# Boundaries between sub-layers: the low part of the first tile's upper half is made by GpSimd between its last two roots and multiplied by TensorE ahead of the last tile's transposes

## The reference

```python
def rmsnorm(x, g):
    xf = x.astype(jnp.float32)
    y = xf * lax.rsqrt(jnp.mean(xf * xf, axis=-1, keepdims=True) + EPS)
    return y.astype(x.dtype) * g

def ffn_sublayer(x, shift, scale, gate, g_pre, g_post, w_in, w_out):
    h = modulate(rmsnorm(x, g_pre), shift, scale)
    a, b = jnp.split(h @ w_in, 2, axis=-1)
    h = (jax.nn.silu(a) * b) @ w_out
    return x + FFN_RES * gate * rmsnorm(h, g_post)
```

## Time and profile before

| what | us |
|---|---|
| median of 3 runs | 3028.7 |
| lowest and highest | 3026.51, 3028.95 |
| the profiled execution | 3027.37 |
| its span in the profile | 3025.3 |
| PE matmuls busy in it | 2971.6 |
| DVE busy | 2194.8 |
| ACT busy | 1152.7 |
| POOL busy | 594.1 |

### The profile page before, as it was taken

One profiled execution on the slowest core, in us unless ns is written; L12 is line 12 of the kernel. 1 busy time (PEld: TensorE's weight loads), 2 busy tenths in 40 slices (PEclk: granted clock), 3 DMA queues, 4 the chain that ended last, 5 costly groups with the idle time before them and its releaser, 6 DMA issues.

```text
span 3025.3 us, 46963 instructions
## 1 busy us (share of the span) xinstructions
PE 2971.6 (98%) x18482; PEld 2753.4 (91%) x18482; DVE 2194.8 (73%) x2831; ACT 1152.7 (38%) x1966; POOL 594.1 (20%) x586
## 2 busy tenths in 40 slices
PE   7999999999999999999999999999999999999999
PEld 6999888999999998999899999979999999888998
DVE  6888678887877656888787576768887888775444
ACT  4222564223322434222422365553224222664222
POOL 1111212112211212112211144541122112211001
PEclk9999999999999999999999999999999999999999
DMA  8666435665665445666566443327675766333443
GB/s 299 209 211 215 142 84 192 209 209 167 210 209 172 117 135 167 219 211 197 181 209 202 132 117 93 105 89 236 208 215 166 221 211 197 111 80 119 126 127 96
DMA packets 565935, 515.61 MB, mean 170 GB/s; under 512 B 43013, under 2 KB 499286, under 8 KB 563926
## 3 DMA queue, kind: packets, MB, share of 16 engines
q1 hardware_dynamic: 565158, 512.37, 55.8%
q10 hardware_dynamic: 560, 0.25, 0.0%
HBM read 509.31 MB, written 3.24 MB: 169 GB/s over the span
## 4 chain that ended last, share of the span: by engine, by line
PE 89%; issue 4%; DVE 2%; POOL 2%; ACT 1%; DMA 1%; SPq 0%; DVEq 0%; POOLq 0%; ACTq 0%
PE bank L1671 19%; PE bank L1673 18%; PE bank L1672 18%; PE bank L1720 9%; PE bank L1722 9%; PE bank L1721 9%; PE bank L1688 2%; PE bank L1695 1%; PE bank L614 1%; PE bank L639 1%; DMA ada_first<-w_ada 1%; PE bank L1753 1%; POOL hg_kr L1491 1%; POOL small L2358 0%; POOL small L2363 0%
## 5 line engine op out<-in xcount | busy, mean ns | idle before, releaser
L1671 PE MATMUL bank<-h_hi,w_hi 128*128 128x384 f32 x3328 | 1120.6, 337 | 0.0
L1673 PE MATMUL bank<-h_hi,w_lo 128*128 128x384 f32 x3328 | 1114.9, 335 | 0.0
L1672 PE MATMUL bank<-h_lo,w_hi 128*128 128x384 f32 x3328 | 1113.6, 335 | 0.0
L1925 ACT ACTIVATE w_hi<-raw 128x1024 fp32r<-128x1024 f32 x646 | 680.8, 1062 | 1032.8 <-PE bank L1673 483.6
L2081 DVE TENSOR_TENSOR w_lo<-raw,w_hi 128x1024 fp32r<-128x1024 f32 x648 | 812.2, 1276 | 330.6 <-ACT w_hi L1925 325.8
L2108 DVE SCALAR_TENSOR_TENSOR fold<-ada_raw,cond,fold 128x1024 f32<-128x1024 f32 x462 | 638.5, 1438 | 0.1
L1671 PEld LDWEIGHTS bank<-h_hi,w_hi 128*128 128x128 f32 x3328 | 625.2, 188 | 10.9 <-ACT tmp L1944 1.6
L1672 PEld LDWEIGHTS bank<-h_lo,w_hi 128*128 128x128 f32 x3328 | 625.3, 188 | 6.1
L1673 PEld LDWEIGHTS bank<-h_hi,w_lo 128*128 128x128 f32 x3328 | 625.0, 188 | 0.0
L2399 POOL TENSOR_TENSOR h_lo<-tmp,h_hi 128x384 fp32r<-128x384 f32 x176 | 280.4, 1593 | 1741.3 <-DVE h_hi L2142 1741.3
L1720 PE MATMUL bank<-w_hi,h_hi 128*128 128x512 f32 x1056 | 415.4, 393 | 0.0
(11 more groups left out here) (204 smaller groups left out, 2425.7 us busy)
## 6 DMA issues: line engine op xcount, KB each, us to landing
raw<-w_ffn_in SPq DMA_DIRECT2D x352, 512.0 KB, 5.0
ada_raw<-w_ada SPq DMA_DIRECT2D x264, 512.0 KB, 4.2
raw<-w_ffn_out SPq DMA_DIRECT2D x176, 512.0 KB, 4.6
raw<-w_hgrn_in SPq DMA_DIRECT2D x40, 512.0 KB, 3.9
g_rows<-g_dram SPq DMA_DIRECT2D x12, 1024.0 KB, 6.7
raw<-w_attn_qkv SPq DMA_DIRECT2D x24, 512.0 KB, 5.9
raw<-w_conv_in SPq DMA_DIRECT2D x24, 512.0 KB, 4.9
ada_first<-w_ada SPq DMA_DIRECT2D x16, 512.0 KB, 10.9
```

Of the source, the lines that this page charges most:

```text
L1671: mm(out, wh, h_hi[:, k, :], start=(k == 0), stop=False)
L1672: mm(out, wh, h_lo[:, k, :], start=False, stop=False)
L1673: last = mm(out, wl, h_hi[:, k, :], start=False, stop=(k == DC - 1))
L1925: A(w_hi[:, b % RING, :], raw[:, b % RAW, :], ACT.Copy).then_inc(w_hi_made, 1)
```

## The change

Three edits, all for the boundaries e = 1 to 11:

- POOL runs `lo_half(e, 0, 1)`, the low part of the upper half of tile 0, between `out_root(e, 2)` and `y_root(e, 2)`. Three `lo_half` remain after the last root, in the order tile 1 upper, tile 0 lower, tile 1 lower.
- PE runs a new `first_low(e)` after `first_tile(e)` and ahead of the transposes of tile 2: it waits for that one low part and does 8 matmuls (2 banks by 4 chunks) of 128 columns, `w_hi` by `h_lo` of tile 0.
- In `first_blocks` the 8 matmuls of the upper half's low part take only tiles 1 and 2 (256 columns) in place of 384. The 8 of the lower half stay at 384.

```diff
             for half in (1, 0):
                 pe.wait_ge(h_lo_made, (NT - 1) * (2 * (s + 1) - half))
                 pe.wait_ge(h_lo_last, 2 * (s + 1) - half)
+                low = rest if half == 1 and s > 0 else slice(0, T)
                 for j, bank in enumerate(banks):
                     for k in range(4 * half, 4 * half + 4):
-                        last = mm(psum[bank][:, 0:T], w_hi[:, (b0 + j) % RING, k * P:(k + 1) * P], h_lo[:, k, :],
+                        last = mm(psum[bank][:, low], w_hi[:, (b0 + j) % RING, k * P:(k + 1) * P], h_lo[:, k, low],
                                   start=False, stop=(k == 3), skip_group_check=True)
...
+        def first_low(s):
+
+            pe.wait_ge(h_lo_made, (NT - 1) * 2 * s + 1)
+            for j, bank in enumerate(first_banks(s)):
+                for k in range(4, 8):
+                    mm(psum[bank][:, 0:P], w_hi[:, (first_block[s] + j) % RING, k * P:(k + 1) * P], h_lo[:, k, 0:P],
+                       start=False, stop=False, skip_group_check=True)
...
                 first_tile(e)
+                first_low(e)
                 turn_normed(e, 2)
...
                 for t in range(NT):
                     out_root(e, t)
+                    if t == NT - 1:
+                        lo_half(e, 0, 1)
                     y_root(e, t)
 
                 gp.wait_ge(h_high_made, 2 * (NT * e + NT - 2) + 2)
-                for half in (1, 0):
-                    for t in range(NT - 1):
-                        lo_half(e, t, half)
+                lo_half(e, 1, 1)
+                lo_half(e, 0, 0)
+                lo_half(e, 1, 0)
```

## The result

| | before | after |
|---|---|---|
| median of 8 runs, us | 3027.85 | 3035.32 |
| lowest and highest | 3024.36, 3029.26 | 3031.17, 3040.16 |
| the profiled execution's span | 3025.3 | 3037.5 |
| PE busy in it | 2971.6 | 2981.4 |
| POOL busy | 594.1 | 587.0 |

What follows compares the result with a forecast made beforehand. PE, busy 98% of the span, bounds the kernel, with a slackless chain from `out_root` to tile 2's transposes at boundaries. Terms -5.0 + 11.2 + 0.6 = +6.8 us on 3028.7 gave 3035.5, range 3028 to 3040.

Steps and rivals of the forecast that it cites:

- Term 2: At each boundary, DVE's additions to y of tile 2 wait for POOL's moved low part: +11.2 us in all.
- the pair at 300.8 us: POOL and DVE subtractions started 0.07 us apart; DVE's took 2.03 us for 1.22, as if begun 0.13 before POOL's end.
- the third pair: At the boundary's end, POOL's subtraction takes 1.75 us for 1.27 and DVE's 1.78 for 0.68, 1.1 more.
- The second: Pair at 58.47 us: POOL takes 1.98 us for some 1.0, DVE's next, at 59.50, 2.03 for 1.28.
- The estimate of 1.24 us: Delay of DVE's addition by the skill page's rule, blocked engine going on about 115 ns after the holder's end.
- rival 1: POOL's low part and DVE's additions don't collide: no delay, 3020.6 to 3023.7 us, faster; chance 0.14.
- rival 2: POOL and DVE share rather than take turns, about 0.5 us delay a boundary: 3029 us, no change; chance 0.12.
- Term 1: Eight low-part matmuls behind L1688 narrowed from 384 to 256 columns: 0.45 us a boundary, -5.0 us, counted in full.
- The 13.85 of the prediction: Time from `first_tile` to L1671 after the change where the clock stays: 13.25 + 1.05 - 0.45 = 13.85 us.
- The end of the boundary: POOL's fourth low part and DVE's `lo_last` disturbed each other, hidden with 0.2 us to spare; nothing gained or lost.
- Term 3: Boundaries with a stretch at PE's lower clock: 3 to 4 expected for 3, +0.6 us, bounds -3.1 and +8.
- rival 3: PE's clock falls in most boundaries, its quiet stretch being later and longer: +13.8 us, 3042.5; chance 0.07.

Runs made afterwards that it cites:

- experiment 1: Kernel before with only GpSimd's order changed, one low part ahead of the last `y_root`, TensorE as before: 3047.33 us, ratio 1.0063 against the kernel before.
- experiment 3: Kernel before with only two of the low part's four chunks made ahead of the last `y_root`, TensorE as before: 3037.56 us, ratio 1.0037.
- experiment 4: Changed kernel, but GpSimd begins the early low part only after both additions to y of tile 2: 3026.69 us, ratio 0.9994 against the kernel before.
- experiment 5: ScalarE's rounding of the sixth weight block moved behind the first Silu in FFN boundaries: 3033.45 us on the changed kernel, 3028.08 on the one before.
- experiment 2: Changed kernel with GpSimd's old order, the 8 added matmuls multiplying the high part instead: 3024.78 us, ratio 0.9991 against the kernel before.

## Why the prediction was right, and where it was not

Forecast 3035.5 with slower the likeliest case, measured 3035.32, slower.

- **Term 2, the delay of the chain,** was +11.2 us, 1.05 a boundary. Measured 5.63 - 4.69 = 0.94 in ten boundaries and 0.59 in the ninth: 10.0 us. The turn was taken as forecast, POOL first. The value worked out from the pair at 300.8 us, 1.0, was nearer than the 1.05 taken between it and the 1.1 of the third pair. Not "all" pairs lie there. The second would have given what was measured: there DVE's instruction ends as if begun at 59.50 + 2.03 - 1.28 = 60.25, 0.20 us before POOL's end at 58.47 + 1.98 = 60.45, and with 0.20 in place of 0.13 the sum gives 0.94. DVE went on 0.21 us before GpSimd's recorded end here. Experiments 1, 3 and 4 show the cause: the delay comes with the low part alone, shrinks by just what POOL's instruction shrinks, and is gone from the addition when POOL starts later. The Trainium skill's rule ("SBUF — State Buffer", section "SBUF: two separate sides"), that the one that starts first holds the shared ports for its whole instruction, agrees with these runs in kind. The estimate of 1.24 us, made with that page's 115 ns, was 0.3 too long; the page gives the 115 ns for GpSimd held up by VectorE, and here it was VectorE that waited.
- **Rivals 1 and 2** (no collision; sharing) are out by the same rows: 1.69 in place of 0.75 in ten boundaries, with POOL's own time unchanged at 1.28.
- **Term 1, the narrower matmuls,** was -5.0 us, 0.45 a boundary, "it counts in full". This step failed in part. From the first low-part matmul to L1671 it was 2.83 us in mixer boundaries on the mean and is 2.35: 0.48 gained, and 13.10 + 0.94 - 0.48 = 13.56 is what was measured (13.54 to 13.56). The 13.85 of the prediction goes by the longer window of the earlier trace rows; up to L1671 it means 13.70. In FFN boundaries at full clock it was 2.89 and is 2.67, 0.22 gained. There PE meets ScalarE's Silu: the four roundings ahead of it start 0.93 us later after `first_tile`'s start, with the chain (9.51 for 8.58 at boundary 2), and experiment 5 shows that one rounding fewer ahead of it gives 0.27 us back. "Where PE never waits, and PE is busy after it" held only for the order of before. At full clock everywhere term 1 would be worth 4 x 0.48 + 7 x 0.22 = 3.5 us.
- **The end of the boundary** I wrote off as nothing gained or lost. Experiment 2 shows what the narrow matmuls would have been worth without the shorter POOL queue at the end: nothing. Term 1 stood on POOL's move.
- **Term 3, the clock,** was +0.6 us, 3 to 4 half-clock boundaries for 3. There are 3 for 3 in the two profiles, and they cost 0.7 to 0.9 us each in place of 0.9 to 1.3 (boundary 9 without its late start), 2.2 in all for 3.1: -0.9, and not +0.6. That the number stayed has a reason not seen: the two halves of the change pull hard in opposite directions. In one profile each: 3 half-clock boundaries of 11 before, 11 with the delay alone, none with the added matmuls alone, 3 with both. So rival 3 is out for the change as a whole, but it is what the delay alone does, and that costs 19.8 us by the medians, not 10.
- That the sum came out within 0.2 us is partly luck. Term 2 was 1.2 too much, term 1 1.5 too much of a gain and term 3 1.5 too much of a loss; -3.5 + 10.0 - 0.9 = +5.6, and the eleven boundaries of the two profiles differ by 5.7. The medians are 7.5 apart, with an interval of about 2.7 us to each side, in which both 5.7 and the forecast 6.8 lie.

## What to carry to other kernels

Before GpSimd work is put in an idle stretch of its own queue, look at what VectorE runs beside it. Here an addition with two operands in SBUF that started 0.13 us after a GpSimd subtraction waited for nearly all of it, 0.94 us of 1.28. If such an addition is on the chain, idle time on GpSimd isn't free. The place two roots earlier, beside nothing with two such operands, turned the same idea from +7.5 us to -8.2, each against the kernel before. And when a step at a wait is shortened, ask for each engine that feeds the next step what slack it has, not only the one that was last.

## What the runs showed of the hardware that I had not expected

- Small fillers on TensorE were worth more by the clock than by their work. Eight matmuls of 128 columns, 0.89 us in an idle stretch of 1.09, took the half-clock boundaries from 3 of 11 to none (experiment 2, with the narrower matmuls behind them), and the same eight beside the delay from 11 to 3. Such a boundary cost 0.5 to 2.2 us here, 2.2 where the mean clock was 0.79. The counts are of one profile each; the mean granted clock over all executions goes the same way, 0.9975 with the fillers alone and 0.991 with the delay alone, where the kernel before has 0.996.
- A lead of 0.13 us was enough to go first: in ten boundaries GpSimd led the addition by 0.13 to 0.14 us and always had its turn before it. In the ninth it led by 0.49, and the addition took 1.35 in place of 1.69, so it is the holder's end that counts, not the overlap.
- DVE went on before GpSimd's recorded end: its addition, 0.75 us alone, ended at 323.14 + 1.69 = 324.83, as if begun at 324.08, 0.21 us before GpSimd's end at 323.01 + 1.28 = 324.29 (0.13 in the earlier trace rows). Sums made with GpSimd's recorded ends were good to about 0.2 us here, no better.
